# Modulation vectors of a two-block transformer kernel: summed on VectorE instead of GpSimd

## The reference, cut to what matters

```python
c_act = jax.nn.silu(c)                                   # c: (1, 1024)
mod = (c_act @ w_ada[l] + b_ada[l]).reshape(B, 3, 3, D)   # w_ada: (1024, 9216)
u = modulate(rmsnorm(h, norm1_g), mod[:,0,0], mod[:,0,1])  # x*(1+scale)+shift
h = h + 0.5 * mod[:,0,2] * swiglu(u, ffn1_w_gu, ffn1_w_down)
u = modulate(rmsnorm(h, norm2_g), mod[:,1,0], mod[:,1,1])
h = h + mod[:,1,2] * mixer(u, ...)
u = modulate(rmsnorm(h, norm3_g), mod[:,2,0], mod[:,2,1])
h = h + 0.5 * mod[:,2,2] * swiglu(u, ffn2_w_gu, ffn2_w_down)
return rmsnorm(h, final_g)
```

## Time and profile before

| what | value |
|---|---|
| median of three runs | 1743.77 us |
| profiled execution, its own time | 1744.57 us |
| its span, first to last instruction | 1742.8 us |
| TensorE busy | 1294.9 us, 74% |
| VectorE busy | 1026.7 us, 59% |
| GpSimd busy | 1021.5 us, 59% |
| ScalarE busy | 390.7 us, 22% |
| mean granted TensorE clock | 0.845 of full speed |
| chain that ended last | PE 54%, DVE 14%, DMA 13%, POOL 9%, issue 6% |

### The profile page before, as it was taken

The page is one execution under the profiler, slowest core; times in us unless marked ns, Lnnn a source line. Parts: engine busy times, 40 slices in busy tenths (PEclk is TensorE's granted clock), DMA queues, the critical chain, the costliest instruction groups (busy, mean ns, idle before and its releaser), DMA issues.

```text
span 1742.8 us, 17930 instructions
## 1 busy us (share of the span) xinstructions
PE 1294.9 (74%) x6189; PEld 923.7 (53%) x6189; DVE 1026.7 (59%) x1761; ACT 390.7 (22%) x663; POOL 1021.5 (59%) x917
## 2 busy tenths in 40 slices
PE   7985699688555545455555576999968888989996
PEld 3433467555222212122222235899868877779995
DVE  2267436885577885455556546665656765354554
ACT  1122321221100220000110012333324250143331
POOL 1488830677766757567777777788878888000000
PEclk9995578899777777677777787999979988989998
DMA  7336302999999979999999993667746555416551
GB/s 244 126 96 229 121 25 82 345 385 372 384 381 378 373 281 384 397 400 382 379 379 339 385 378 117 206 194 272 229 159 215 164 180 182 144 52 214 168 193 61
DMA packets 179706, 435.41 MB, mean 250 GB/s; under 512 B 13881, under 2 KB 84610, under 8 KB 179638
## 3 DMA queue, kind: packets, MB, share of 16 engines
q0 software_dynamic: 84384, 306.26, 47.0%
q1 hardware_dynamic: 94214, 126.18, 21.8%
q10 hardware_dynamic: 1040, 2.10, 0.3%
HBM read 433.44 MB, written 2.14 MB: 250 GB/s over the span
## 4 chain that ended last, share of the span: by engine, by line
PE 54%; DVE 14%; DMA 13%; POOL 9%; issue 6%; ACT 2%; SPq 0%; DVEq 0%; ACTq 0%; POOLq 0%
PE quad L1302 12%; PE quad_a L1257 8%; PE quad L1257 6%; PE quad_a L1316 6%; DMA arena<-in_peer_v_dram,arena 6%; PE quad_a L1053 5%; POOL ring L727 4%; POOL arena L727 4%; PE quad_a L1384 4%; DMA ring<-in_peer_v_dram,arena 3%; PE quad_a L1442 2%; PE quad_a L1450 2%; DMA ring<-in_ffn_w_gu_dram 2%; DMA ring<-in_peer_u_dram,arena 1%; PE quad_a L1148 1%
## 5 line engine op out<-in xcount | busy, mean ns | idle before, releaser
L1257 PE MATMUL quad_a<-arena 128*128 128x512 f32 x384 | 202.2, 690 | 155.5 <-DMA arena<-in_peer_v_dram,arena 155.5
L1257 PE MATMUL quad<-ring,arena 128*128 128x512 f32 x360 | 186.5, 681 | 130.2 <-DMA ring<-in_peer_v_dram,arena 130.2
L1257 PEld LDWEIGHTS quad_a<-arena 128*128 128x128 f32 x384 | 84.5, 226 | 273.3 <-issue 273.0
L727 POOL DMA_INDIRECT ring<-in_peer_u_dram,arena x136 | 138.6, 1019 | 146.1 <-DVE arena L1768 71.6
L680 POOL TENSOR_TENSOR arena<-arena 128x512 f32<-128x512 f32 x144 | 205.5, 1427 | 18.7 <-POOL arena L680 11.0
L1687 DVE TENSOR_TENSOR w_lo<-ring,w_hi 128x2048 fp32r<-128x2048 f32 x66 | 165.1, 2509 | 77.4 <-ACT w_hi L897 77.3
L1302 PE MATMUL quad<-u_hi,w_hi 128*128 128x256 f32 x704 | 201.0, 286 | 10.7 <-DVE u_lo L1894 5.5
L1257 PEld LDWEIGHTS quad<-ring,arena 128*128 128x128 f32 x360 | 77.8, 221 | 235.6 <-issue 235.6
L1302 PE MATMUL quad<-u_lo,w_hi 128*128 128x256 f32 x704 | 200.8, 285 | 0.0
L1302 PE MATMUL quad<-u_hi,w_lo 128*128 128x256 f32 x704 | 200.5, 285 | 0.0
L1787 DVE CUSTOM_DVE_ANT_0 arena<-ring,quad 128x1024 f32<-128x1024 f32 x128 | 155.2, 1220 | 30.1 <-DMA ring<-in_peer_u_dram,arena 22.5
(11 more groups left out here) (304 smaller groups left out, 2416.1 us busy)
## 6 DMA issues: line engine op xcount, KB each, us to landing
ring<-in_ffn_w_gu_dram SPq DMA_DIRECT2D x44, 1024.0 KB, 9.1
arena<-in_w_ada_dram POOLq DMA_DIRECT2D x48, 512.0 KB, 4.4
ring<-in_ffn_w_down_dram SPq DMA_DIRECT2D x22, 1024.0 KB, 5.0
ring<-in_w_mix_in_dram SPq DMA_DIRECT2D x20, 1024.0 KB, 5.4
ring<-in_w_ada_dram POOLq DMA_DIRECT2D x24, 512.0 KB, 4.0
arena<-in_peer_w_query_dram SPq DMA_DIRECT2D x4, 2048.0 KB, 8.4
arena<-in_w_in_dram SPq DMA_DIRECT2D x3, 2048.0 KB, 11.1
arena<-in_w_out_dram SPq DMA_DIRECT2D x2, 2048.0 KB, 13.3
```

Source lines behind the costliest of these rows:

```text
L727: gp.indirect_dma_start(out=rows_of(n), out_offset=None, in_=t["peer_" + kind][0], in_offset=bass.IndirectOffsetOnAxis(ap=expert[tt][:, sl ...
L1257: last = te.matmul(sum_side[tt][:, cols], diag[:, i % DIAGS], rows_of(n)[:, cols], start=(slot == pe_slots[0]), stop=(slot == pe_slots[-1] ...
```

## The change

GpSimd no longer does arithmetic for the sums. It clears the sums, loads the biases, and issues 72 loads of `w_ada`, each one k-block by 1024 columns (128 rows of 4 KB, 0.5 MB), into four buffers. VectorE does one `scalar_tensor_tensor` for each: `sum = block * c_act[:, k] + sum`, 128x1024. VectorE's 72 sums stand in its program as follows: 24 in the head (4 before the `fill` copies, 10 after `c_row_ready`, 6 after the sums of squares of dk, 4 after those of dq), 32 in FFN 0 (from tile 2 on, one or two behind each tile: two behind tiles with j mod 5 in 0, 2, 4), 8 in the mixer (one behind each split 2 to 7, one behind two of the `ya` products), 8 in FFN 1. The sums for the gate of s=2 now end in FFN 1: TensorE adds them over the partitions before its last two down products, and only "columns" is left before the norm of s=2. VectorE's loop over the blocks is written out in place of a hardware loop.

```diff
-ADA_W = 256
...
-        late = area(arena, B0 + 3 * D, 4 * D + D)
...
+        LATE = 27680
+        ada_sum = [[area(arena, B0 + 7168, D), area(arena, B0 + 7168 + D, D), gate1]]
+        ada_sum.append([area(arena, LATE + 4096 + m * D, D) for m in range(3)])
+        ada_sum.append([gates[2], ada_sum[1][1], ada_sum[1][2]])
+        ADA = [(s, m, k) for s in range(2) for k in range(KD) for m in range(3)] + [(2, m, k) for m in range(3) for k in range(KD)]
+        ADA_BUFS = 4
+        ada_head = [area(ring, at, D) for at in (0, D, 2 * D, 9984)]
+        ada_late = [area(arena, LATE + D * i, D) for i in range(ADA_BUFS)]
...
+            def load_ada(*loads):
+                for n in loads:
+                    s, m, k = ADA[n]
+                    if n >= ADA_BUFS:
+                        pool.wait_ge(ada_used.sem, n - ADA_BUFS + 1)
+                    src = t["w_ada_2"][0, k * P:(k + 1) * P, (3 * s + m) * D:(3 * s + m + 1) * D]
+                    gp.dma_start(ada_buf(n), src).then_inc(ld_ada[n % ADA_BUFS], 16)
...
+            begin_sums(*((0, m) for m in range(3)))
+            pool.wait_ge(d_full.sem, d_at["nT", 2, 1] + 1)
+            load_ada(*range(ADA_BUFS))
             bias_ready.step(pool, gp.memset(mask, 0.0))
...
+            load_ada(*range(ADA_BUFS, 10))
             pool.wait_ge(ld_bias, 32)
...
-            def sum_ada(s, m, i, half):
...
-            pool.wait_ge(c_ready.sem, 1)
-            modulation(0)
-
+            load_ada(*range(10, 24))
             pool.wait_ge(d_full.sem, d_at["wo", 1, 1] + 1)
...
-            for s in (1, 2):
-                modulation(s)
-                final_scale(s)
+            begin_sums((1, 0), (1, 1), (1, 2), (2, 0))
+            load_ada(*range(24, 56))
+            final_scale(1)
+            pool.wait_ge(ada_full.sem, len(ADA_JOBS))
+            begin_sums((2, 1), (2, 2))
+            load_ada(*range(56, 68))
+            final_scale(2)
+            load_ada(*range(68, 72))
...
-            ada_out(2)
+            ada_out(2, "columns")
             norm_part(2)
             silu_part(1)
+            ada_out(2, 0, 1)
             norm_part(3)
...
+            def modulation(s, *jobs):
+                pe.wait_ge(ada_used.sem, ada_count(s, jobs == ("columns",)))
+                for job in jobs:
+                    ada_full.mark(over_partitions(psum[ADA_BANK[job]], s, job))
...
                     down(j - 2, (j - 2) % 4, 4)
+                if f:
+                    modulation(2, 0, 1)
                 down(20, 0, 5)
...
-            modulation(2)
+            modulation(2, "columns")
+            pe.wait_ge(ada_free.sem, len(ADA_JOBS) + 1)
...
+            def sum_ada(count):
+
+                for _ in range(count):
+                    n = ada_next[0]
+                    s, m, k = ADA[n]
+                    if n == 0:
+                        ve.wait_ge(c_ready.sem, 1)
+                    if (s, m) not in ada_at:
+                        ve.wait_ge(ld_ada_bias, 16 * (3 if s == 0 else 7 if s == 1 or m == 0 else 9))
+                    else:
+                        ve.wait_ge(ada_used.sem, ada_at[s, m] + 1)
+                    ve.wait_ge(ld_ada[n % ADA_BUFS], 16 * (n // ADA_BUFS + 1))
+                    ada_used.mark(v.scalar_tensor_tensor(out=ada_sum[s][m], in0=ada_buf(n), scalar=c_act[:, k:k + 1], in1=ada_sum[s][m],
+                                                         op0=ALU.mult, op1=ALU.add))
+                    ada_next[0], ada_at[s, m] = n + 1, n
...
-            ve.wait_ge(ada_ready.sem, 1)
...
+                def tile_and_sums(j, c):
+                    tile(j, c)
+                    if f == 0 and j >= 2:
+                        sum_ada(2 if j % 5 in (0, 2, 4) else 1)
+                    elif f and 2 <= j < 18 and j % 2 == 0:
+                        sum_ada(1)
+                each_block(v, tile_and_sums, lo_slot(f), written=True)
...
-            split_mix(*range(2, 8))
+            for n in range(2, 8):
+                split_mix(n)
+                sum_ada(1)
```

More of the change, by code:

```diff
@@ L243, in program, with ada_buf, ada_count @@
         mod = sb("mod", 3 * 2 * KD)[:].rearrange("p (s m k) -> p s m k", s=3, m=2)
[L245 to L249 removed]
+        LATE = 27680
[6 more added lines that the diff above has]
+        ada_late = [area(arena, LATE + D * i, D) for i in range(ADA_BUFS)]
+        def ada_buf(n):
+            return (ada_late if ADA[n][0] else ada_head)[n % ADA_BUFS]
+        def ada_count(s, columns):
+            return 24 * s + (24 if s < 2 else 16 if columns else 24)
         uT = area(arena, 0, KD * SEQ).rearrange("p (k n) -> p k n", k=KD)
@@ L483, in mix_hi_of, with each_block @@
             return mix_hi[{14: "conv", 15: "sgb"}.get(n, ("conv", "qk")[n % 2])]
-        def each_block(eng, tile, split):
+        def each_block(eng, tile, split, written=False):
             def both(i, parity, last=False):
@@ L496, in each_block @@
                 both(0, parity)
-            with eng.Fori(1, 5) as i:
-                for parity in range(2):
-                    both(i, parity)
+            if written:
+                for i in range(1, 5):
+                    for parity in range(2):
+                        both(i, parity)
+            else:
+                with eng.Fori(1, 5) as i:
+                    for parity in range(2):
+                        both(i, parity)
             both(5, 0, last=True)
@@ L683, in modulation @@
-            def modulation(s):
-                for half in range(2):
-                    load_ada(s, 0, 0, half)
-                if s == 2:
-                    pool.wait_ge(ada_full.sem, len(ADA_JOBS))
-                for m in range(3):
-                    gps.step(pool, gp.memset(ada_sum[s][m], 0.0))
-                    gp.dma_start(ada_sum[s][m][0:1], t["b_ada_2"][:, (3 * s + m) * D:(3 * s + m + 1) * D]).then_inc(ld_ada_bias, 16)
-                pool.wait_ge(ld_ada_bias, 16 * 3 * (s + 1))
-                for m in range(3):
-                    in_loop = CHUNKS if m < 2 else CHUNKS - 1
-                    with gp.Fori(0, in_loop) as i:
-                        for half in range(2):
-                            sum_ada(s, m, i, half)
-                            pool.sem_inc(gps_go, 1)
-                            load_ada(s, m, i + 1, half)
-                    if m == 2:
-                        for half in range(2):
-                            sum_ada(s, m, CHUNKS - 1, half)
-                    gps.sent += 2 * CHUNKS * ADA_OPS
-                ada_ready.mark(gp.tensor_copy(small[:, 255:256], ada_sum[s][2][:, 0:1]))
@@ L1550, in _ @@
                 half_heads("dk", tt, C_DK, None)
+            sum_ada(6)
             for tt in range(3):
@@ L1993, in _ @@
                     x_dve.step(ve, v.tensor_tensor(gate_, gate_, two, ALU.mult))
+                    if name == "ya" and n in (1, 3):
+                        sum_ada(1)
                     if name == "yb":
```

64 lines of the change are left out of this document (26 added, 38 removed).

## The result

The changed kernel takes 1684.16 us (median of 4 runs, 1681.58 to 1686.44) against 1741.12 us of the kernel before, run beside it (4 runs, 1738.1 to 1749.57). The ratio is 0.9673, with a 95% interval of 0.9648 to 0.9698: faster, and by more than forecast.

A forecast was written before the change was run, and what follows sets the result against it. It took GpSimd's arithmetic to block VectorE, which is the chain in the rotary heads. Terms -18.3 - 4 - 3 + 0 - 10 - 2.5 = -37.8 from 1744.6 gave 1706.8, stated as 1707, range 1687 to 1731.

The forecast's parts named there:

- The price of the sums: VectorE's 72 sums at 1.285 us are 92.5 us, taken as mostly fitting beside other work or into waits.
- The rotary heads: Five tiles on VectorE's chain, 33.8 us, shrink to 15.5 once GpSimd no longer blocks it: -18.3.
- The head before 120 us: 24 sums fit into VectorE's waits; about 4 us of cover left despite late loads 10 to 13: price 0.
- Rival 3: GpSimd doesn't cause the stretching, so VectorE gains no speed and only the gate move is left: 1742, chance 0.07.
- Rival 5: Head late: loads 10 to 13 miss the cover by 8 us, ScalarE's root holds TensorE's banks: 1715, chance 0.10.
- the trap of the Trainium skill: Two-port VectorE instructions lengthen DMA issues from 0.62 to 3.1 us; loads 10 to 13 come 10 late, sum 6 higher.
- Rival 4: Attention: with a shorter rotary stretch TensorE's clock stays at 2.4 GHz, half of 24 us gained: 1695, chance 0.10.
- Rivals 1 and 2: FFN 0: loads and sums cost 20 us, 1727, chance 0.13; or 76 less 8, slower than before, 1775, chance 0.05.
- Mixer: -10: Splits 6 and convolution 7.9 less a sum's 1.3 give 12.6, four fifths taken; from 0 to -13.
- FFN 0: "0": Ten blocks at 0.8 us for new sums and loads, 8, cancel today's waits; from -6 to +20.
- Gate of s=2: "-2.5": Moving gate sums takes 4 from the norm of s=2 and adds 1.5 before FFN 1's last down products.
- Gather: 0: The expert gather, 744 us of the span, has no stretching and isn't touched by the change.

The follow-up runs named there:

- a1: Kernel before, with each of GpSimd's four operations per chunk cut from 256 columns of the sums to 4: 1685.4 us, ratio 0.9683.
- a3: Changed kernel, with 20 sets of GpSimd's old arithmetic put back on unused data from about 95 us on, in the head: 1719.28 us, ratio 0.988.
- a4: Changed kernel, with GpSimd's old arithmetic put back on unused data in FFN 0 and the mixer: 1728.66 us, ratio 0.9925.
- a2: Changed kernel, with each of VectorE's 72 sums cut to 8 of its 1024 columns: 1683.29 us, 0.9 below the changed kernel.
- c1: Changed kernel with FFN 0's sums moved ahead of the pieces' landing, plus unneeded matmuls in TensorE's waits of the rotary heads: 1680.0 us, ratio 0.9645.
- b3: Kernel before, with seven unneeded 128x512 matmuls in TensorE's wait for the convolution: 1740.68 us, ratio 0.9981; ya to w_out 59.5 to 56.9.
- b2: Changed kernel, with the gate sums back ahead of the norm of s=2: 1688.17 us; that norm 17.9 against 16.0, FFN 1 192.0 against 189.7.
- c3: Changed kernel with FFN 0's sums moved ahead of the pieces' landing, plus unneeded matmuls in TensorE's waits of the three norms: 1670.28 us, ratio 0.9594.
- d1: Changed kernel, FFN 0's sums moved, with unneeded matmuls in rotary heads, attention steps and norms: 1714.92 us against 1787.41 for the kernel before, ratio 0.9597.

## Why the prediction was right in its mechanism and too small in its sum

**Right, and shown.** VectorE was held up by GpSimd's arithmetic. a1 takes the arithmetic away and a3 and a4 put it back, both with the effect and each in the stage where it was put. The price of the sums, 72 x 1.28 us, is nearly all hidden (a2's 0.9). The rotary heads came out as worked out, 18.3, and with them the choice to read 1.37 and 1.74 of the earlier trace rows as blocked lengths: unblocked they are 0.42 and, for the two, 0.89. The head before 120 us had its cover of 4 us, although the loads there took 5.5 and not 4.4. Rival 3 falls by the 0.96 in all tiles. Rival 5 falls by the root at 84.62, and with it the time that the trap of the Trainium skill would have given (loads 10 to 13 were issued while VectorE was idle, so the rule itself wasn't tried). Rival 4 falls by the clock over the whole attention, 0.64 before and 0.63 after, and by c1. Rivals 1 and 2 were about FFN 0, which became shorter.

**The step that failed: "Mixer: -10 ... 12.6 in all, of which I take four fifths, since TensorE's projections and ScalarE's rounding come next in line."** Nothing came next. From the end of FFN 0 to ya it was 19.3; of that 3.6 lies ahead of the mixer's first product, at the norm, and 15.7 in the mixer. TensorE's idle time in the mixer fell by 12.9, which is all of the 12.6 and not four fifths of it. The convolution's 7.9 was well sized: its wait of 8.3 is gone, not shortened. The wait for the scores gave 2.2 (8.2 to 6.0), that for a split 1.8 (8.5 to 6.7), a short one 0.6. The forecast had named none of the three as a wait; its own way, five splits at 1.2 less the sum of 1.3, gives 4.7 for what they show as 4.6. The other 2.8 us are TensorE's busy time on the same products, which goes with the granted clock, 0.89 before and 0.94 after. The forecast had no term for it.

**The step that was missing: what a wait costs behind itself.** The sum priced waits by their length alone, and the clock stood only in a rival, for the attention. ya to w_out has -2.6 by the clock alone (b3), and the mixer the 2.8 above. FFN 0 in a4 shows the same term at its largest, 12.7 us on top of 21.2 of waits.

**FFN 0: "0", measured -3.5.** Both terms were seen. The removal, 6 to 8 as worked out, is worth 7.0, waits and the products behind them; sums and loads were mis-sized, 8 against the 3.5 that they cost (a1).

**Gate of s=2: "-2.5", measured -6.0.** The norm's -4 came out, but with the gate back in its place b2 is only 1.9 longer: its gate products took 1.96 us at the high clock, not 3.54 as in the earlier trace rows. The other half, "+1.5" in FFN 1, has the wrong sign. TensorE in order of time at the end of FFN 1:

```profile
1662.20 1.88 PE L1214 MATMUL quad<-arena,ones 128*128 128x512 f32 x4
1664.31 0.70 PE L1315 MATMUL quad_a<-w_hi,h_hi 128*128 128x512 f32 x2 [0.23 <-DVE w_lo L1704]
```

The gate's matmuls take the place of the 2.0 us wait of the earlier trace rows: they cost 1.88 and leave 0.23, and the pairs of down products behind take 0.70 and then 0.62 us. In the kernel before, behind its wait, they took

```profile
1720.80 0.86 PE L1316 MATMUL quad_a<-w_hi,h_hi 128*128 128x512 f32 x2 [1.95 <-DVE w_lo L1687]
1721.46 1.05 PE L1316 MATMUL quad_a<-w_lo,h_hi 128*128 128x512 f32 x2
```

The gate's matmuls are fillers, as in b3. FFN 1 with them is 189.7 to 190.8 in eight kernels (188.3 in c3 and d1, which have fillers at the norms too), without them 191.7 to 192.3 in four.

**Gather: 0, measured -3.2.** Kernels with the same gather lie between 781.4 and 791.9, d1 apart. It is scatter, so 3 us of the total are luck, as much as the time lies below the range.

The forecast's terms sum to 37.8 us and the stages to 58.1. Of the 20.3 between them, the mixer's 5.7, ya to w_out's 2.6, the gate's 3.5, FFN 0's 3.5 and the gather's 3.2 are 18.5. All of them went one way, so a range built from separate terms ended 3 us too high. At least 5.4 of them, the mixer's 2.8 and ya to w_out's 2.6, are products at a higher granted clock; that the errors of the gate and of FFN 0 have a share of the same cause is likely and wasn't measured apart.

## What to carry to other kernels

Arithmetic that reads SBUF on GpSimd isn't free beside a VectorE that is on the chain; ask of each stage how long the same VectorE instruction takes where GpSimd is silent, and move or shrink what GpSimd reads before you tune VectorE's order. Price a wait of TensorE twice, as its length and as the products behind it at the lower granted clock, and where a wait can't be removed, try a few matmuls that nobody needs in it. Errors of terms that share a cause add up in one direction, so widen the range on that side.

## What the runs showed of the hardware that was not expected

- GpSimd's memsets don't touch VectorE's two-source instructions (0.96, 2.290 and 1.279 us as without them), nor a reduction of 128x1088 (1.286), but take a scaling of 128x4 from 0.170 to 0.564 us. A reciprocal right behind such a scaling is recorded as longer too (0.170 to 0.406) without being held itself.
- Seven matmuls in a wait of 8.3 us, with 2.35 us of it left idle, kept the granted clock at 1.00; without them it was 0.52 in the six microseconds behind the wait. Fillers in the rotary heads kept it at 1.00 there, and it was 0.51 in the attention behind them.
- The same gather took 781 to 792 us in thirteen profiles and 839 us in that of d1, beside which the kernel before was 46 us longer as well.
